# Two groups of seven products instead of one in nine of ten tile pairs, with one of the sums on GpSimd and the residual kept in DRAM

## The chip, the cores and the metric

The kernel runs on one core of one Trainium2 chip. The metric is the device time of one execution in microseconds. The kernel before takes 963.92 us (median of three runs, 963.87 to 964.64).

## The reference, cut to what matters

The reference is one layer of a decoder: sparse attention, a layer norm, a SwiGLU feed-forward part and a second layer norm, for 256 tokens of 2048 features, all in float32.

```
x = LN(alpha*x + mixer(x))                                   # attention, not touched by the change
x = LN(alpha*x + (silu(x @ w_gate) * (x @ w_up)) @ w_down)   # w_gate, w_up: 2048 x 5632; w_down: 5632 x 2048
```

The change concerns `x @ w_gate` and `x @ w_up` (and, by its buffers, the start of `@ w_down`).

## The kernel before, in words

**Three matmuls for one product.** TensorE multiplies in a reduced float32 format (fp32r). To keep the precision, each operand is split into a high part (a rounded copy) and a low part (operand minus high part), and a product is made of three matmuls: high by high, high by low, low by high. So every piece of weights passes two engines before TensorE can use it: the scalar engine (ACT) writes the high part `w_hi` from the loaded `raw`, then the vector engine (DVE) writes `w_lo = raw - w_hi`. Both work on halves of 128 x 1024 elements. `w_hi` and `w_lo` are rings of four halves: ACT may write half n when TensorE has used half n - 4. All halves are counted through the whole kernel (`hi_done`, `lo_done`, `pe_used`).

**Tiles and pairs.** The 5632 hidden columns are cut into 22 tiles of 256; a tile's gate and up columns stand side by side, 512 columns. Tiles 0 and 1 are made alone (`first_tile`, `tile_1`). Tiles 2 to 21 are made in ten pairs, p = 1 to 10, by `pair(p)` on TensorE, `hi_pair(p)` on ACT and `lo_pair(p)` on DVE. The features are 16 blocks of 128 rows (k tiles).

**Seven products for eight.** For the first four k tiles of a pair, two token halves by two k tiles by two column tiles are taken as a 2 x 2 block product and made with seven products instead of eight (Strassen's scheme in Winograd's form). One half then holds one factor for two such block products ("quads"), and TensorE makes 6 matmuls from it (2 quads by 3). The seven weight factors are b11, T1 = b11 + b12, T2 = T1 + b22, b21, T3 = b12 + b22, b22 and T4 = T2 + b21 (signs by the layout); the four sums are made by DVE in place in `raw` (`t_sum`, L1254), two quads at once. The factors of the tokens' side (`s_t`) are made once, before pair 1, by GpSimd (POOL, L1387 to L1398) and ACT (L831). The other twelve k tiles are "plain": 12 halves of 12 matmuls each. So a pair is 7 + 12 = 19 halves and 7 x 6 + 12 x 12 = 186 matmuls of 512 columns, L1769 (`strassen`) and L1782 (`plain`). Between the products ACT copies partial sums from one PSUM bank to another (`seed`, L851, three in a pair, and L871).

**Work of the tiles.** For each tile ACT applies silu (L816), DVE multiplies by the up part (`gate_up`, L1224), TensorE transposes the result (`turn_hid`, L1738, 4 small matmuls), ACT and DVE split it (`hid_hi` L820, `hid_lo` L1228). In the pairs this stands at fixed places between the halves.

**Loads.** All weights come by the SP engine's DMA queue, in program order, each after a wait on `lo_done`. `raw` has five slots of 2048 elements (two halves). In tile 0, tile 1 and the last matrix slots 0 to 3 are a ring; in the pairs slots 0 to 2 are the plain ring and slots 3 and 4 hold the two quads. The quads of pair 1 wait until DVE has split the last half of tile 1, since slot 3 is still in use by it (the row `DMA raw<-in_w_pairs` in the rows below). The residual stream `xn` stays in SBUF.

**The last matrix.** `hid @ w_down` follows the pairs in four column groups of 24 halves, L1561 on TensorE.

The order on each engine is written out by hand. Within an engine nothing is reordered: an instruction whose wait is open holds up all that stands behind it.

## Time and profile before

| | us |
|---|---|
| median of three runs | 963.92 |
| the profiled execution's own time | 964.98 |
| its span, first to last instruction | 962.8 |
| TensorE (PE) busy in the span | 949.2 |
| DVE busy | 624.6 |
| ACT busy | 486.4 |
| POOL busy | 52.2 |
| mean granted TensorE clock | 0.991 |

A matmul's record overlaps the next one's, so a busy share of 99% tells that TensorE hardly ever waits, and not that each record's length is its cost: the cost of one matmul is read from the chain, where a run of matmuls stands as one piece with its count. The chain that ended last runs from the start of the pairs to the end almost wholly over TensorE.

### The profile page before, as it was taken

How to read it: one execution, taken by the hardware profiler on the slowest of the kernel's cores; microseconds unless marked ns; L12 is line 12 of the kernel's file. 1: busy time of each engine (PE TensorE's matmuls, PEld its weight loads, DVE VectorE, ACT ScalarE, POOL GpSimd, SP SyncE). 2: the span in 40 equal slices, each digit the busy share in tenths (PEclk: the TensorE clock that was granted, in tenths of full speed). 3: DMA queues.
4: the chain of work that ended last, by engine and by line, in shares of the span. 5: the costliest groups of instructions: out<-in, count | busy, mean ns of one | idle time of the engine just before them, and what ended most of it. 6: DMA issues, size and time to landing. Idle time of an engine off the chain costs nothing.

```text
span 962.8 us, 11466 instructions
## 1 busy us (share of the span) xinstructions
PE 949.2 (99%) x4536; PEld 794.4 (83%) x4536; DVE 624.6 (65%) x750; ACT 486.4 (51%) x644; POOL 52.2 (5%) x49
## 2 busy tenths in 40 slices
...
GB/s 364 315 136 175 122 55 214 180 392 88 132 87 262 124 270 166 228 197 152 235 115 268 136 253 185 208 216 133 164 206 288 172 220 180 170 225 168 219 131 88
DMA packets 28147, 183.84 MB, mean 191 GB/s; under 512 B 3136, under 2 KB 3648, under 8 KB 8640
## 3 DMA queue, kind: packets, MB, share of 16 engines
...
q8 instruction: 36, 0.59, 0.2%
q14 instruction: 15, 0.12, 0.0%
q0 software_dynamic: 32, 0.00, 0.0%
...
## 4 chain that ended last, share of the span: by engine, by line
PE 70%; DVE 1%; DMA 0%; ACT 0%; issue 0%; DVEq 0%; ACTq 0%
PE acc L1782 26%; PE acc L1561 25%; PE tp L1782 8%; PE acc L1769 6%; PE tp L1769 4%; PE tp L1738 1%; DMA raw<-in_w_pairs 0%; DVE raw L1254 0%; PE acc L1867 0%; DVE w_lo L1090 0%; DVE w_lo L1242 0%; ACT w_hi L836 0%; ACT w_hi L755 0%; DVE stats L1326 0%; ACT acc L851 0%
## 5 line engine op out<-in xcount | busy, mean ns | idle before, releaser
L1090 DVE TENSOR_TENSOR w_lo<-raw,w_hi 128x1024 fp32r<-128x1024 f32 (+1 forms) x123 | 146.1, 1195 | 133.8 <-ACT w_hi L755 133.1
L1782 PE MATMUL acc<-w_hi,act_t 128*128 128x512 f32 x720 | 227.1, 392 | 0.0
L1561 PE MATMUL acc<-w_hi,hid_t 128*128 128x512 f32 x672 | 207.9, 389 | 0.0
L1249 DVE TENSOR_TENSOR w_lo<-raw,w_hi 128x1024 fp32r<-128x1024 f32 x120 | 145.2, 1224 | 95.8 <-ACT w_hi L845 94.7
L755 ACT ACTIVATE w_hi<-raw 128x1024 fp32r<-128x1024 f32 x116 | 115.9, 1001 | 164.7 <-PE acc L1561 152.3
L845 ACT ACTIVATE w_hi<-raw 128x1024 fp32r<-128x1024 f32 x120 | 126.1, 1060 | 126.3 <-PE acc L1782 111.2
L1782 PEld LDWEIGHTS acc<-w_hi,act_t 128*128 128x128 f32 x720 | 135.2, 188 | 27.8
L1561 PEld LDWEIGHTS acc<-w_hi,hid_t 128*128 128x128 f32 x672 | 126.1, 188 | 26.1
L1782 PE MATMUL acc<-w_lo,act_t 128*128 128x512 f32 x360 | 140.2, 389 | 0.0
L1561 PE MATMUL acc<-w_lo,hid_t 128*128 128x512 f32 x336 | 130.7, 389 | 0.0
L836 ACT ACTIVATE w_hi<-raw 128x1024 fp32r<-128x1024 f32 x70 | 72.9, 1057 | 74.4 <-DVE raw L1254 48.5
L1242 DVE TENSOR_TENSOR w_lo<-raw,w_hi 128x1024 fp32r<-128x1024 f32 x70 | 83.9, 1222 | 35.1 <-ACT w_hi L836 34.0
L1782 PEld LDWEIGHTS acc<-w_lo,act_t 128*128 128x128 f32 x360 | 67.7, 188 | 13.6
L1782 PE MATMUL tp<-w_hi,act_t 128*128 128x512 f32 x240 | 74.7, 389 | 0.0
L1561 PEld LDWEIGHTS acc<-w_lo,hid_t 128*128 128x128 f32 x336 | 63.1, 188 | 13.1
L1561 PE MATMUL acc<-w_hi,o_t 128*128 128x512 f32 x224 | 73.4, 398 | 0.0
L1782 PEld LDWEIGHTS tp<-w_hi,act_t 128*128 128x128 f32 x240 | 45.1, 188 | 9.3
L1561 PEld LDWEIGHTS acc<-w_hi,o_t 128*128 128x128 f32 x224 | 42.1, 188 | 8.6
L1254 DVE TENSOR_TENSOR raw<-raw 128x1024 f32<-128x1024 f32 x40 | 47.9, 1219 | 0.0
L1782 PE MATMUL tp<-w_lo,act_t 128*128 128x512 f32 x120 | 46.7, 389 | 0.0
L1561 PE MATMUL acc<-w_lo,o_t 128*128 128x512 f32 x112 | 43.6, 390 | 0.0
L1769 PE MATMUL acc<-w_hi,act_t 128*128 128x512 f32 x100 | 36.9, 410 | 6.6 <-DVE w_lo L1242 6.6
...
## 6 DMA issues: line engine op xcount, KB each, us to landing
raw<-in_w_pairs SPq DMA_DIRECT2D x80, 1024.0 KB, 4.7
raw<-in_w_down SPq DMA_DIRECT2D x32, 1024.0 KB, 4.6
raw<-in_w_out SPq DMA_DIRECT2D x16, 1024.0 KB, 4.8
...
raw<-in_w_gu SPq DMA_DIRECT2D x8, 1024.0 KB, 7.0
...
raw<-in_w_uq SPq DMA_DIRECT2D x4, 1024.0 KB, 6.3
raw<-in_w_ukv SPq DMA_DIRECT2D x4, 1024.0 KB, 5.7
```

The lines of the kernel that those rows point to most:

```text
L755: act.activation(w_hi[:, (2 * slot + half + shift) % RING, 0:n], raw[:, slot, first:first + n], ACT.Copy).then_inc(hi_done, 1)
L836: act.activation(by_quad(w_hi[:, v_pair(p, n) % RING, :]), quad(block), ACT.Copy).then_inc(hi_done, 1)
L845: act.activation(w_hi[:, v_pair(p, n) % RING, :], raw[:, slot, h % 2 * HALF:(h % 2 + 1) * HALF], ACT.Copy).then_inc(hi_done, 1)
L1090: dve.tensor_tensor(w_lo[:, h, 0:n], raw[:, slot, first:first + n], w_hi[:, h, 0:n], ALU.subtract).then_inc(lo_done, 1)
L1242: dve.tensor_tensor(by_quad(w_lo[:, v % RING, :]), quad(block), by_quad(w_hi[:, v % RING, :]), ALU.subtract).then_inc(lo_done, 1)
L1249: dve.tensor_tensor(w_lo[:, v % RING, :], raw[:, h // 2 % PAIR_RING, h % 2 * HALF:(h % 2 + 1) * HALF], w_hi[:, v % RING, :], ALU.subtract) ...
L1254: dve.tensor_tensor(quad(dst), quad(x), quad(y), ALU.add).then_inc(t_done, 1)
L1561: last = pe.matmul(acc[:, bank0 + t, :], lhs[:, k, x, t * P:(t + 1) * P], part[:, w, n * GC:(n + 1) * GC], start=(start and x == 0 and par ...
L1738: last = pe.transpose(turned[:, c, t * P:(t + 1) * P], hid[:, t, c * P:(c + 1) * P], ident[:])
L1769: last = pe.matmul(out, factor(q, what, x), part[:, v % RING, q * GC:(q + 1) * GC], start=(start and (q, x) == (0, 0) and part is w_hi), s ...
L1782: last = pe.matmul(out[:, t, :], act_t[:, k0 + m, x, t * P:(t + 1) * P], part[:, v % RING, m * GC:(m + 1) * GC], start=False, stop=((h % P ...
```

## The change

Pairs 2 to 10 take two groups of four k tiles by the seven products; pair 1 keeps one group (`GROUPS_OF`). A pair of two groups has 14 product halves and 8 plain halves, 22 halves and 14 x 6 + 8 x 12 = 180 matmuls. For each factor the halves of group 0 and group 1 follow each other.

`raw` has six slots: two hold plain halves, four at a time and each with a semaphore of its own (`plain_full`), the other four hold the quads. The two quads of pair 1 go to slots 4 and 5, which tile 1 doesn't use, and their loads have no wait. From pair 2 the quads of the next pair are loaded one by one between plain halves 4 to 7 of the pair before.

GpSimd makes T3 = b12 + b22 in place (`t3_sums`, L1456 of the new kernel), once for each group, after DVE's T1; DVE makes the other three sums of each group (L1312). The tokens' factors of the second group are made in the plain part of pair 1 (`factors_hi(1)` and GpSimd's loop).

`s_t` is twice as large and lies where `xn` lies. `xn` is stored to the DRAM of the output before `s_t` is written (`x1_stored`, waited for by ACT), and loaded back after the products of pair 10 (`x1_back`, waited for by DVE in column group 1 of the last matrix).

In a pair, `turn_hid(2p-2)` moves from the start of the plain part to behind the first product half, `turn_hid(2p-1)` to the start of the plain part; ACT's and DVE's work on the tiles (`hid_chores`) moves to halves 5, 5G+4 and the last of the pair (G is the number of groups).

```diff
-QUADS = 2
-PAIR_K = 2 * QUADS
+QUADS = 4
 B11, B21, B12, B22 = range(4)
+T1, T2, T4 = range(3)
...
+GROUPS_OF = (None, 1) + (2,) * (PAIRS - 2)
 PRODUCTS = 7
-PLAIN = (KD - PAIR_K) // 2
-PAIR_HALVES = PRODUCTS + 2 * PLAIN
-PAIR_RING = 3
-PLAIN_LOADS = PLAIN
-PAIR_SIGNALS = PAIR_HALVES - 2
+PLAIN_SLOTS = 4
...
-        raw = sb("raw", [P, PAIR_RING + QUADS, RAW_ELEMS])
+        raw = sb("raw", [P, PLAIN_SLOTS // 2 + QUADS, RAW_ELEMS])
...
+        s_t = nc.alloc_sbuf_tensor_at("s_t", [P, 2, 4, QUADS, P], F32R, offset=base_x)
...
-        s_t = sb("s_t", [P, 2, 4, QUADS, P], F32R)
...
-                if p > 1:
-                    sp.wait_ge(lo_done, v_pair(p - 1, PRODUCTS))
-                for q in range(QUADS):
-                    if p == 1 and q == 0:
-                        sp.wait_ge(lo_done, V_FFN + 2 * TILE_HALVES)
-                    sp.dma_start(raw[:, PAIR_RING + q, :],
-                                 w_pairs[p - 1][:, q * RAW_ELEMS:(q + 1) * RAW_ELEMS])\
-                      .then_inc(raw_full[PAIR_RING + q], 16)
+            def load_quad(p, n):
+
+                q = quad_slots(p)[n]
+                if p == 1:
+                    pass
+                elif p == 2 and q < 2:
+                    sp.wait_ge(lo_done, V_FFN + TILE_HALVES + 2 * (PLAIN_SLOTS // 2 + q) + 2)
+                else:
+                    sp.wait_ge(lo_done, v_pair(p - 1, products(p - 1)))
+                sp.dma_start(raw[:, PLAIN_SLOTS // 2 + q, :], w_pairs[p - 1][:, n * RAW_ELEMS:(n + 1) * RAW_ELEMS])\
+                  .then_inc(quad_full[q], 16)
...
-                if n >= PAIR_RING:
-                    sp.wait_ge(lo_done, v_pair(p, PRODUCTS + 2 * (n - PAIR_RING) + 2))
-                elif p > 1:
-                    sp.wait_ge(lo_done, v_pair(p - 1, PRODUCTS + 2 * (n + PAIR_RING) + 2))
+                m = PLAIN_BEFORE[p] + n
+                if m < PLAIN_SLOTS:
+                    sp.wait_ge(lo_done, V_FFN + TILE_HALVES + m + 1)
                 else:
-                    sp.wait_ge(lo_done, V_FFN + TILE_HALVES + 2 * n + 2)
-                e0 = (QUADS + n) * RAW_ELEMS
-                sp.dma_start(raw[:, n % PAIR_RING, :], w_pairs[p - 1][:, e0:e0 + RAW_ELEMS])\
-                  .then_inc(raw_full[n % PAIR_RING], 16)
...
+                    sp.wait_ge(lo_done, plain_v(m - PLAIN_SLOTS) + 1)
+                e0 = 2 * GROUPS_OF[p] * RAW_ELEMS + n * HALF
+                sp.dma_start(plain_raw(m), w_pairs[p - 1][:, e0:e0 + HALF]).then_inc(plain_full[m % PLAIN_SLOTS], 16)
...
+                if isinstance(g, int) and n < 2:
+                    sp.wait_ge(lo_done, v_pair(PAIRS - 1, products(PAIRS - 1)))
+                elif isinstance(g, int) and n < RING:
+                    sp.wait_ge(lo_done, V_DOWN - PLAIN_SLOTS + 2 * slot + 2)
                 else:
                     sp.wait_ge(lo_done, V_DOWN + 2 * (n - RING) + 2)
...
+            load_quad(1, 0)
+            load_quad(1, 1)
+            for n in range(PLAIN_SLOTS):
+                load_plain(1, n)
+            sp.wait_ge(x1_done, TOK * CHUNKS)
+            sp.dma_start(a["out"].rearrange("(t p) d -> p t d", p=P), xn[:]).then_inc(x1_stored, 16)
+            for p in range(1, PAIRS):
+                if p > 1:
+                    for n in range(PLAIN_SLOTS):
+                        load_plain(p, n)
+                for n in range(PLAIN_SLOTS, plain_halves(p)):
+                    load_plain(p, n)
+                    if p < PAIRS - 1:
+                        if n - PLAIN_SLOTS < 2 * GROUPS_OF[p + 1]:
+                            load_quad(p + 1, n - PLAIN_SLOTS)
+                    elif n - PLAIN_SLOTS < 2:
+                        load_down(0, n - PLAIN_SLOTS)
+
+            for b in range(2, RING):
                 load_down(0, b)
+            sp.wait_ge(x1_stored, 16)
+            sp.wait_ge(*used_half(v_pair(PAIRS - 1, products(PAIRS - 1))))
+            sp.dma_start(xn[:], a["out"].rearrange("(t p) d -> p t d", p=P)).then_inc(x1_back, 16)
...
+            def factors_hi(g):
+
+                act.wait_ge(x1_stored, 16)
+                act.wait_ge(s_step, 5 * g + 5)
+                act.activation(s_t[:, 0, :, 2 * g:2 * g + 2, :], s_sum[:, g, :, :, :], ACT.Copy).then_inc(s_hi, 1)
...
 
...
+                G, n_products = GROUPS_OF[p], products(p)
+                seeds = {G + 3: (0, first[:, 0, :], 1.0), 3 * G + 3: (2, second[:, 0, :], -1.0),
+                         5 * G + 3: (4, first[:, 1, :], 1.0)}
+                for j in range(halves(p)):
+                    if j in seeds:
+                        if j == G + 3:
+                            act.wait_ge(ffn_hid, 2 * p - 1)
+                        seed(p, *seeds[j])
+                    if j == 2 * G + 4:
+                        if p > 1:
+                            act.wait_ge(p5_added, 2 * (p - 1))
+                        act.wait_ge(*used_half(v_pair(p, 2 * G - 1)))
+                        act.activation(p5_s[:], tp[:, 2, :], ACT.Copy).then_inc(p5_done, 1)
+                    if j < n_products:
+                        hi_product(p, j // G, j % G)
+                    else:
+                        hi_plain(p, j - n_products)
+                    if j == 5:
                         if p > 1:
                             hid_hi(2 * p - 2)
                         silu_step(2 * p - 1)
-                    if h == 9:
+                    if j == 5 * G + 4:
                         hid_hi(2 * p - 1)
+                    if j == n_products + plain_halves(p) // 2 + 3:
                         silu_step(2 * p)
+                    if p == 1 and j == n_products + 6:
+                        factors_hi(1)
...
+            def t_sum(p, g, dst, x, y):
+                dve.tensor_tensor(quad(p, g, dst), quad(p, g, x), quad(p, g, y), ALU.add).then_inc(t_done, 1)
+
+            def hid_chores(p, j):
+
+                if j == 5:
+                    if p > 1:
+                        hid_lo(2 * p - 2)
+                    gate_up(2 * p - 1)
+                if j == 5 * GROUPS_OF[p] + 4:
+                    hid_lo(2 * p - 1)
+                if j == products(p) + plain_halves(p) // 2 + 3:
+                    gate_up(2 * p)
...
+                groups = range(GROUPS_OF[p])
+                for n in range(PRODUCTS):
+                    for g in groups:
+                        lo_product(p, n, g)
+                        if n == 0:
+                            t_sum(p, g, B11, B11, B12)
+                        if n == 3:
+                            t_sum(p, g, B21, B11, B21)
+                        hid_chores(p, GROUPS_OF[p] * n + g)
+                    for g in groups:
+                        if n == 1:
+                            t_sum(p, g, B11, B11, B22)
+                for h in range(plain_halves(p)):
                     lo_plain(p, h)
-                    if h == 3:
...
+                    hid_chores(p, products(p) + h)
+                    if h == 2:
                         dve.wait_ge(p5_done, p)
...
+                    if g == 1 and h == 2:
+                        dve.wait_ge(x1_back, 16)
...
+            def t3_sums(p):
+
+                for g in range(GROUPS_OF[p]):
+                    pool.wait_ge(t_done, T_BEFORE[p] + g + 1)
+                    pool.tensor_tensor(quad(p, g, B12), quad(p, g, B12), quad(p, g, B22), ALU.add).then_inc(t3_done, 1)
...
+            for g in range(2):
+                if g == 1:
+                    pool.wait_ge(lo_done, v_pair(1, products(1)))
+                k = act_t[:, 4 * g:4 * g + 4, :, :].rearrange("p (q k) x s -> p q k x s", q=2)
+                x1, s_g = x1_t[:, g, :, :, :], s_sum[:, g, :, :, :]
+                pool.tensor_tensor(x1, k[:, :, :, 0, :], k[:, :, :, 1, :], ALU.add).then_inc(s_step, 1)
...
+                pool.wait_ge(s_hi, g + 1)
+                pool.tensor_tensor(s_t[:, 1, :, 2 * g:2 * g + 2, :], s_g, s_t[:, 0, :, 2 * g:2 * g + 2, :],
+                                   ALU.subtract).then_inc(s_lo, 1)
+                if g == 0:
+                    t3_sums(1)
+            for p in range(2, PAIRS):
+                t3_sums(p)
...
-                v = v_pair(p, n)
-                pe.wait_ge(lo_done, v + 1)
-                for q in range(QUADS):
-                    for x, part in ((0, w_hi), (0, w_lo), (1, w_hi)):
-                        last = pe.matmul(out, factor(q, what, x), part[:, v % RING, q * GC:(q + 1) * GC],
-                                         start=(start and (q, x) == (0, 0) and part is w_hi),
-                                         stop=((q, x) == (QUADS - 1, 1)), skip_group_check=not start)
-                last.then_inc(pe_used, 1)
+                for g in range(GROUPS_OF[p]):
+                    v = v_pair(p, GROUPS_OF[p] * n + g)
+                    if v == v_pair(p, 1) and p > 1:
+                        turn_hid(2 * p - 2)
+                    pe.wait_ge(lo_done, v + 1)
+                    for n_q in range(2):
+                        for x, part in ((0, w_hi), (0, w_lo), (1, w_hi)):
+                            end = (g, n_q, x) == (GROUPS_OF[p] - 1, 1, 1)
+                            last = pe.matmul(out, factor(2 * g + n_q, what, x),
+                                             part[:, v % RING, n_q * GC:(n_q + 1) * GC],
+                                             start=(start and (g, n_q, x) == (0, 0, 0) and part is w_hi),
+                                             stop=end, skip_group_check=not start)
+                    last.then_inc(pe_used, 1)
...
-                pe.wait_ge(s_lo, 1)
+                pe.wait_ge(s_lo, min(p, 2))
...
-                for h in range(PLAIN):
-                    if h == 0 and p > 1:
-                        turn_hid(2 * p - 2)
-                    if h == 5:
+                n = plain_halves(p) // 2
+                for h in range(n):
+                    if h == 0:
                         turn_hid(2 * p - 1)
                     plain(p, h, first)
```

The order on DVE, from the end of pair 2 into pair 3 (the first L1242 begins pair 3), before. L1242 is the low part of a product half, L1254 a sum, L1249 the low part of a plain half, L1228 `hid_lo` and L1224 `gate_up`:

```order
L1249 TENSOR_TENSOR w_lo<-raw,w_hi 128x1024
L1242 TENSOR_TENSOR w_lo<-raw,w_hi 128x1024
L1254 TENSOR_TENSOR raw<-raw 128x2x512 x2
L1242 TENSOR_TENSOR w_lo<-raw,w_hi 128x1024
L1254 TENSOR_TENSOR raw<-raw 128x2x512
L1242 TENSOR_TENSOR w_lo<-raw,w_hi 128x1024 x2
L1254 TENSOR_TENSOR raw<-raw 128x2x512
L1242 TENSOR_TENSOR w_lo<-raw,w_hi 128x1024 x3
L1249 TENSOR_TENSOR w_lo<-raw,w_hi 128x1024 x4
L1228 TENSOR_TENSOR hid_t<-tp,hid_t 128x2x256
L1224 TENSOR_TENSOR hid<-hid,tp 128x512
```

The same place of the new kernel, the end of pair 2 into pair 3; L1301 is the low part of a product half, L1312 a sum, L1308 the low part of a plain half, L1285 `hid_lo` and L1281 `gate_up`:

```order
L1308 TENSOR_TENSOR w_lo<-raw,w_hi 128x1024 x5
L1281 TENSOR_TENSOR hid<-hid,acc 128x512
L1301 TENSOR_TENSOR w_lo<-raw,w_hi 128x1024
L1312 TENSOR_TENSOR raw<-raw 128x2x512
L1301 TENSOR_TENSOR w_lo<-raw,w_hi 128x1024
L1312 TENSOR_TENSOR raw<-raw 128x2x512
L1301 TENSOR_TENSOR w_lo<-raw,w_hi 128x1024 x2
L1312 TENSOR_TENSOR raw<-raw 128x2x512 x2
L1301 TENSOR_TENSOR w_lo<-raw,w_hi 128x1024 x2
L1285 TENSOR_TENSOR hid_t<-tp,hid_t 128x2x256
L1281 TENSOR_TENSOR hid<-hid,tp 128x512
L1301 TENSOR_TENSOR w_lo<-raw,w_hi 128x1024
```

DVE had four sums among seven product halves, with the work on the tiles behind four plain halves; now it has six among fourteen, and one `hid_lo` and one `gate_up` stand behind the sixth product half.

The SP queue before, from the first loads of the pairs; L521 is a quad and L534 a plain slot of two halves:

```order
L534 DMA raw<-in_w_pairs 128x2048 x3
L521 DMA raw<-in_w_pairs 128x2048 x4
L534 DMA raw<-in_w_pairs 128x2048 x6
L521 DMA raw<-in_w_pairs 128x2048 x2
L534 DMA raw<-in_w_pairs 128x2048 x6
```

The same queue of the new kernel; L559 is a quad, L570 one plain half, L589 the store of `xn`:

```order
L559 DMA raw<-in_w_pairs 128x2048 x2
L570 DMA raw<-in_w_pairs 128x1024 x4
L589 DMA out<-xn 128x2x2048
L570 DMA raw<-in_w_pairs 128x1024
L559 DMA raw<-in_w_pairs 128x2048
L570 DMA raw<-in_w_pairs 128x1024
L559 DMA raw<-in_w_pairs 128x2048
L570 DMA raw<-in_w_pairs 128x1024
L559 DMA raw<-in_w_pairs 128x2048
L570 DMA raw<-in_w_pairs 128x1024
L559 DMA raw<-in_w_pairs 128x2048
L570 DMA raw<-in_w_pairs 128x1024 x9
```

The two quads of pair 1 moved ahead of the plain halves, the store stands behind four of these, and a pair's quads alternate with plain halves, each of which waits for a `lo_done` of its own.

## Rows read from the trace of the kernel before

**Rows 1.** The page: the span, and each engine's busy time.

```profile
span 962.8 us, 11466 instructions
PE 949.2 (99%) x4536; PEld 794.4 (83%) x4536; DVE 624.6 (65%) x750; ACT 486.4 (51%) x644; POOL 52.2 (5%) x49
```

**Rows 2.** The chain of waits in time order: start, us, what. Pairs 1, 2, 10.

```profile
283.60 9.79 PE acc L1769 x30
293.39 13.60 PE acc L1782 x60
...
326.50 4.08 PE tp L1769 x18
...
350.12 0.44 PE tp L1738 x4
...
714.64 2.72 PE acc L1561 x12
```

**Rows 3.** Windows: us, busy of PE, PEld, DVE, ACT, POOL, clock, DMA share, GB/s.

```profile
412.75:455.88 43.13, 43.13 (x196) 35.70 (x195) 30.88 (x29) 23.61 (x28) 0.00 (x0) 1.00 0.51 195
269.99:276.56 6.57, 0.00 (x1) 0.04 (x1) 1.38 (x2) 1.06 (x1) 0.00 (x0) 0.67 0.49 205
276.56:289.30 12.74, 11.49 (x25) 8.12 (x26) 11.39 (x10) 7.60 (x10) 0.00 (x0) 0.50 0.00 0
425.00:426.00 1.00, 1.00 (x6) 0.81 (x5) 0.86 (x2) 0.42 (x1) 0.00 (x0) 1.00 1.02 434
```

**Rows 4.** Timeline of DVE into pair 4, whose first matmul starts at 412.75.

```profile
405.81 1.23 DVE L1242 TENSOR_TENSOR w_lo<-raw,w_hi 128x1024 fp32r<-128x1024 f32 x1 [1.58 <-ACT w_hi L836]
406.95 2.35 DVE L1254 TENSOR_TENSOR raw<-raw 128x1024 f32<-128x1024 f32 x2
409.30 1.23 DVE L1242 TENSOR_TENSOR w_lo<-raw,w_hi 128x1024 fp32r<-128x1024 f32 x1
...
412.78 2.36 DVE L1242 TENSOR_TENSOR w_lo<-raw,w_hi 128x1024 fp32r<-128x1024 f32 x2 [1.13 <-ACT w_hi L836]
```

**Rows 5.** Timeline of ACT there: halves, a seed, a tile's split and silu.

```profile
404.71 1.06 ACT L836 ACTIVATE w_hi<-raw 128x1024 fp32r<-128x1024 f32 x1 [1.74 <-PE acc L1782]
408.20 1.06 ACT L836 ACTIVATE w_hi<-raw 128x1024 fp32r<-128x1024 f32 x1 [2.43 <-DVE raw L1254]
...
414.21 0.58 ACT L851 ACTIVATE acc<-tp 128x512 f32<-128x512 f32 x1 [0.35 <-PE tp L1769]
...
423.28 0.58 ACT L820 ACTIVATE hid_t<-tp 128x512 fp32r<-128x512 f32 x1
423.76 0.59 ACT L816 ACTIVATE hid<-acc 128x512 f32<-128x512 f32 x1
```

**Rows 6.** Timeline of DVE in tile 1 and of `hid_lo`.

```profile
243.85 3.32 DVE L1090 TENSOR_TENSOR w_lo<-raw,w_hi 128x1024 fp32r<-128x1024 f32 x1 [0.26 <-ACT w_hi L755]
...
252.13 0.67 DVE L1224 TENSOR_TENSOR hid<-hid,acc 128x512 f32<-128x512 f32 x1
...
262.42 0.69 DVE L1228 TENSOR_TENSOR hid_t<-tp,hid_t 128x512 fp32r<-128x512 f32 x1 [4.13 <-ACT hid_t L820]
264.31 2.58 DVE L1090 TENSOR_TENSOR w_lo<-raw,w_hi 128x1024 fp32r<-128x1024 f32 x1 [1.20 <-ACT w_hi L755]
```

**Rows 7.** Timeline of POOL: four in a row, then beside tile 1.

```profile
69.22 10.04 POOL L1372 TENSOR_TENSOR more_lo<-raw,more_hi 128x1024 fp32r<-128x1024 f32 x4 [41.06 <-DVE score L1025]
...
243.68 2.41 POOL L1387 TENSOR_TENSOR x_t<-act_t 128x1024 f32<-128x1024 f32 x1 [112.39 <-DVE act_t L1172]
246.16 1.60 POOL L1391 TENSOR_TENSOR s_sum<-x_t 128x256 f32<-128x256 f32 x1
...
263.41 2.40 POOL L1398 TENSOR_TENSOR s_t<-s_sum,s_t 128x1024 fp32r<-128x1024 f32 x1 [10.61 <-ACT s_t L831]
```

**Rows 8.** Timeline of ACT in tile 1: the high part of `s_t`.

```profile
262.28 1.05 ACT L831 ACTIVATE s_t<-s_sum 128x1024 fp32r<-128x1024 f32 x1
```

**Rows 9.** The page: DMA issues, KB each, median us to landing.

```profile
raw<-in_w_pairs SPq DMA_DIRECT2D x80, 1024.0 KB, 4.7
```

More of the change, by code:

```diff
@@ L747, in _, with hi_loop @@
                     hi_static(SPLIT_OF[s])
-            def hi_loop(used, raw_count, half, slot, n=HALF, first=None, shift=0):
+            def hi_loop(used, raw_count, half, slot, n=HALF, first=None):
                 first = half * n if first is None else first
@@ L1811, in pair @@
                 pe.wait_ge(p5_added, 2 * p)
-                for h in range(PLAIN, 2 * PLAIN):
+                for h in range(n, 2 * n):
                     plain(p, h, second)
```

258 lines of the change are left out of this document (114 added, 144 removed).

## The prediction

> **What bounds the kernel now.** I read the page first: TensorE is busy 949.2 of 962.8 us, DVE 624.6, GpSimd 52.2 [rows 1]. Its records overlap, so next comes the chain of waits: from 283.60 on it is TensorE alone. 18 matmuls take 4.08 us, 0.2267 each; a product half (6) is 1.36 and a plain half (12) 2.72; four transposes take 0.44 [rows 2]. Pairs 2 to 10 run from 326.50 to 714.64, nine of 43.13 us: 186 x 0.2267 = 42.17, and two times 0.44; TensorE never waits there. The window of one such pair shows DVE busy 30.88 of 43.13 us and ACT 23.61 [rows 3]: shares that say little of the product part, where TensorE needs a half every 1.36 us and DVE also makes sums.
>
> The windows before pair 1 show the other loss: TensorE stands for 6.57 us, the granted clock goes from 2.4 to 1.2 GHz, and stays there until about 289.3, after 12.7 us of pair 1 [rows 3]. The wait is for pair 1's quads, loaded only when tile 1's last half is split. From the end of tile 1 (269.99) to the first plain half (283.60 + 9.79 = 293.39) pass 23.4 us [rows 2].
>
> The timelines give the steps. Back to back DVE takes 1.14 a step (406.95 to 409.30 for two sums, less 0.07 of overlap), 1.23 alone [rows 4]. An ACT half takes 1.06; it starts 0.12 after TensorE frees the place (half 0 of pair 4: 412.75 - 3 x 2.72 = 404.59, start 404.71) and 0.03 after a sum (408.20) [rows 5]. Seed, `hid_hi` and silu take 0.5 to 0.6 each [rows 5], `hid_lo` and `gate_up` 0.65 each [rows 6].
>
> **The change, part by part.**
>
> TensorE: nine pairs lose 6 matmuls, 54 x 0.2267 = 12.2 us. A pair without a stall would take 180 x 0.2267 + 0.88 = 41.7 us.
>
> Pair 1: its quads are loaded early, so the 6.57 us wait and the slow clock go. What is late next: the low part of tile 1's last half, which starts at 264.31 and ends at 266.89 [rows 6]. DVE then makes half 0 (to 268.0) and T1 (269.1); ACT's half 1 lasts to 270.2, GpSimd's T3 from 269.15 to 271.55, DVE's half 1 ends at 272.65, T2 at 273.8, ACT's half 2 at 274.9 and half 3 at 275.9, the seed that product 2 waits for at 276.5. TensorE starts half 2 there, 3.8 us late, half 4 at 279.7, 0.4 late, and ends half 6 near 284: 23.4 becomes 14, a gain of 9.4 us if the clock holds.
>
> The store of `xn`: ACT's write of `s_t`, at 262.28 [rows 8], now waits for it. It is issued when DVE has split four halves of tile 1, at about 252.2 (`gate_up` starts at 252.13 behind them) [rows 6]; 2 MB at 434 GB/s [rows 3] behind up to 0.5 MB take 6, and landing takes about 2.2 more than moving (4.7 less 2.5 for 1 MB) [rows 9]: 260 to 261. I price it at 0, with 2 us as the upper end. Behind that ACT instruction stands tile 1's last half. The load back has 2.1 MB and stands in SP's queue ahead of the second norm's rows; DVE waits for it a column group later, tens of us. Cost 0, at most 5.
>
> DVE and GpSimd in pairs 2 to 10: here is the price. GpSimd's operation of 128 x 1024 takes 2.40 to 2.41 us with DVE on small operations or on big ones [rows 7]. DVE's does not keep its time: started at 243.85 it took 3.32 us and ended 1.08 after GpSimd's 243.68 + 2.41; that of 264.31 took 2.58 and ended 1.08 after GpSimd's 263.41 + 2.40 [rows 6, 7]. So DVE stood until GpSimd was done. The reverse holds too: a GpSimd step of a quarter of the size took 1.60 at 246.16, while DVE finished its own [rows 7]. `gate_up`, which reads PSUM, took 0.67 at 252.13, as always [rows 6]. The weight splits and the sums all read SBUF twice, so a sum on GpSimd costs DVE up to 2.4 us, where DVE's own sum costs 1.14. For two in a pair: between 0 (they fall in DVE's idle time) and 4.8 us. I take them where they fall in the order.
>
> The Trainium skill, page SBUF — State Buffer, section Who interferes with whom, says that a DVE instruction with two SBUF inputs and a GpSimd instruction that reads SBUF exclude each other, and whoever issues first blocks the other for its whole length. The rows above agree (2.58 for 1.23). By it the whole 2.40 counts; were the port shared half and half, each sum would cost DVE about 1.2 us, and the time would be some 20 us lower. Its page Perfetto Trace Analysis, section Optimizing Scalar/DVE Operations, warns of moving work between these two for this reason.
>
> Now a pair of two groups, time 0 at its first matmul, DVE as in rows 4 at first. Half 0's low part ends at -5.7, T1a at -4.6. GpSimd takes T3a from -4.5 to -2.1, so half 1 ends at -1.0, T1b at 0.1. Half 2 is ready and goes first, to 1.3. T3b runs to 3.7, half 3 ends at 4.7, T2a at 5.9, T2b at 7.0, half 4 at 8.2. TensorE wants half 3 at 4.5 and half 4 at 6.2: stalls of 0.3 and 2.1. Half 5 follows at 9.8 (ACT has a seed first), then `hid_lo` and `gate_up` to 11.0, half 6 at 12.1, T4a, half 7 at 14.4, T4b, half 8 at 16.7. TensorE starts them at 12.2, 14.5 and 16.8, stalls of 1.0, 0.9 and 0.9, plus 0.2 at half 5. From there DVE needs 1.14 a half and TensorE 1.36. The products end at 25.0 for 19.5: 5.5 us of stall. Then `turn_hid` stands at the start of the plain part, ACT waits for it with `hid_hi` and plain half 1 behind it; its low part is ready 0.25 late. Pair: 41.7 + 5.5 + 0.25 = 47.4 us.
>
> From pair 3 loads add to it. In the second part of a pair SP issues 6 MB, each plain half after a `lo_done`; at 434 GB/s they need 14 us and start at 23.5. The last plain half lands near 39.1, where ACT could take it at 36.7; DVE begins the next pair 1.4 us later, misses the idle time before it, and all that follows shifts: 48.8 us. Without this it is 47.4, the other end.
>
> Sum: pair 2 47.4 and eight of 48.8 make 437.8, less 9 x 43.13 = 388.2: +49.6. With pair 1, -9.4: +40.2. On the profiled execution's 964.98 that is 1005.2; the median of the runs lies 1.06 below that execution: 1004.
>
> **The rivals.**
>
> GpSimd's sums cost DVE nothing (they meet its idle time or start behind it). Then half 4 ends at 6.1, `hid_lo` and `gate_up` still hold half 6 until 10.2, and T4a, T4b make halves 7 and 8 late: 0.3 + 1.1 + 0.85 + 0.9 = 3.2 us of stall, with 0.25 behind it: 45.2 a pair, 9 x 2.07 = 18.6, less 9.4, +9: 973. Against it: rows 6 and 7. For it: before the pair DVE does have idle time (1.58 and 1.13 us) [rows 4].
>
> The clock falls in the stalls. For: it fell 2.3 us into the gap before pair 1, by the 0.67 of the 6.57 us [rows 3]. Against: the longest stall here is 2.1 us, and 1.36 us of matmuls lie between. If 1.2 GHz then stays for 12.7 us as in rows 3, halves 4 to 8 take 2 x 1.275 = 2.55 each, to 21.0 instead of 18.2: 2.8 a pair, 25 us: 1029.
>
> DVE keeps up, and it is faster. From the start of half 0's low part (-6.94) to TensorE's start of the last product half (18.1) are 25.0 us, and DVE's 14 halves, 6 sums, `hid_lo` and `gate_up` need 20 x 1.14 + 1.3 = 24.1. If DVE could run that far ahead, the pairs save 12.2, with pair 1 21.6: 942. Against it: four places in the ring, so half 3 can't begin before time 0; DVE would have to have its sums before that, but the order puts T2a and T2b behind half 3. It decides from about 1 us of stall a pair.
>
> **How the numbers follow.** The forecast 0.62 (993 to 1018, by one more or less us a pair and the two prices of the loads); no cost from GpSimd 0.15; the clock 0.15; DVE keeps up 0.05; the rest, between the first two, 0.03. The range 976 to 1028 leaves out the last us of the clock's case, most of the 973 case and the fast one. A measurement tells 0.2% (1.9 us) from no change. Faster 0.05, within 0.2% 0.02, slower 0.93.
>
> **What would show it.** Right: PE's waits for the low part of product halves, about 50 us over the nine pairs, most before halves 4, 6, 7, 8; DVE's longest splits near 2.3 to 3.5 us beside GpSimd's sums; 14 us from tile 1's end to the plain halves at full clock; pairs of 47 to 49 us. Wrong: pairs near 41.7 us, or DVE splits of 1.23 throughout, or clock 0.5 in the products of each pair.

## The result, and the profile after

The changed kernel takes 1012.48 us (median of 4 runs, 1011.13 to 1013.63), the kernel before in the same session 963.89 (4 runs, 963.78 to 964.64). The ratio is 1.0503, with a 95% interval of 1.0486 to 1.0519: 5% slower. The forecast was 1004 us with a range of 976 to 1028.

The page of the changed kernel, to be read against [rows 1]: the span, the busy times, and the shares of the chain that ended last.

```profile
span 1010.7 us, 11576 instructions
PE 955.5 (95%) x4482; PEld 782.0 (77%) x4482; DVE 713.1 (71%) x794; ACT 509.3 (50%) x672; POOL 123.7 (12%) x74
PE 66%; DVE 23%; DMA 6%; ACT 3%; issue 2%; ACTq 0%; DVEq 0%
```

TensorE has the 54 matmuls less, and yet the span is 47.9 us longer. DVE is busy 88.5 us more; the chain, almost wholly TensorE's before [rows 2], now goes to DVE for 23% (1% before) and to transfers for 6%. Where they stand in it, pair 1 and, from the end of pair 4, pair 5:

```profile
287.38 27.25 PE acc L1868 x120
...
464.68 3.33 DVE raw L1312
468.02 4.46 DVE w_lo L1301 x2
484.44 8.41 PE acc L1853 x36
499.62 7.86 DMA raw<-in_w_pairs
```

(Start, us, what, as in rows 2.) The pattern of DVE, DVE, PE and DMA comes back in each of the pairs 3 to 9, and without the DMA in pair 10.

Four of the ten pairs as windows (columns as in rows 3): pairs 2, 3, 5 and 10.

```profile
319.89:367.52 47.63, 43.56 (x189) 34.02 (x188) 39.02 (x35) 26.02 (x30) 5.95 (x2) 1.00 0.45 177
367.52:416.62 49.10, 44.83 (x189) 35.27 (x188) 40.17 (x35) 26.21 (x30) 6.30 (x3) 0.97 0.44 172
466.05:515.35 49.30, 43.63 (x189) 33.94 (x188) 40.64 (x35) 26.03 (x30) 6.76 (x3) 1.00 0.43 171
713.33:762.32 48.99, 44.84 (x189) 35.34 (x188) 38.51 (x34) 25.79 (x30) 3.83 (x2) 0.97 0.40 151
```

Pair 2 takes 47.63 us, pairs 3 to 10 from 48.99 to 50.10; the nine end 442.4 us after pair 2's start, where before they took 388.2 (nine of 43.13 [rows 3]). That is +54.2. Pair 1 gives back 6.4: the first matmul of pair 2 starts at 319.89 instead of 326.34. Together +47.8, the 47.9 of the spans.

Where TensorE stands in pair 5, from its timeline (start, us, engine, line, operation; in brackets the idle time before it and what ended that):

```profile
472.53 0.50 PE L1853 MATMUL tp<-w_hi,s_t 128*128 128x512 f32 x1 [1.62 <-DVE w_lo L1301]
476.11 0.47 PE L1853 MATMUL acc<-w_hi,s_t 128*128 128x512 f32 x1 [1.92 <-DVE w_lo L1301]
479.80 0.50 PE L1853 MATMUL acc<-w_hi,act_t 128*128 128x512 f32 x1 [0.67 <-DVE w_lo L1301]
482.07 0.51 PE L1853 MATMUL acc<-w_hi,act_t 128*128 128x512 f32 x1 [0.61 <-DVE w_lo L1301]
484.44 0.47 PE L1853 MATMUL acc<-w_hi,s_t 128*128 128x512 f32 x1 [0.71 <-DVE w_lo L1301]
```

Each wait is for the low part of a product half (3, 4, 6, 7 and 8), 5.53 us in sum. The idle time understates them: starts of matmuls are 0.2267 apart elsewhere, and against that pace each stall costs 0.16 more than its bracket, and the start behind it comes about 0.1 late again. So counted, the five cost 6.8 us. Waits too short to be listed, above all 0.4 at the second plain half, bring it to 7.4, and 41.7 + 7.4 = 49.1 of the pair's 49.30.

The cause on DVE, and the same stretch on GpSimd (POOL):

```profile
461.19 1.22 DVE L1301 TENSOR_TENSOR w_lo<-raw,w_hi 128x1024 fp32r<-128x1024 f32 x1
462.33 1.22 DVE L1312 TENSOR_TENSOR raw<-raw 128x1024 f32<-128x1024 f32 x1
463.47 1.22 DVE L1301 TENSOR_TENSOR w_lo<-raw,w_hi 128x1024 fp32r<-128x1024 f32 x1
464.60 3.42 DVE L1312 TENSOR_TENSOR raw<-raw 128x1024 f32<-128x1024 f32 x1
467.94 4.54 DVE L1301 TENSOR_TENSOR w_lo<-raw,w_hi 128x1024 fp32r<-128x1024 f32 x2
```

```profile
463.63 3.31 POOL L1456 TENSOR_TENSOR raw<-raw 128x1024 f32<-128x1024 f32 x1 [41.57 <-DVE raw L1312]
468.10 3.30 POOL L1456 TENSOR_TENSOR raw<-raw 128x1024 f32<-128x1024 f32 x1 [1.16 <-DVE raw L1312]
```

GpSimd's first sum starts behind DVE's T1, while DVE is in the split that began at 463.47; DVE's next operation begins at 464.60. The sum ends at 466.94, 2.34 after that, so it lasts 3.31 instead of its usual 2.40 [rows 7], as if it had first waited for DVE. DVE's next sum, begun at 464.60, ends at 468.02, 1.08 after GpSimd's end, in 3.42 instead of 1.22. The two splits behind take 4.54 instead of 2.35 beside the second sum. Against its own times DVE loses 2.2 + 2.2 = 4.4 us in this pair, where making the two sums itself would cost 2 x 1.14 = 2.3.

The end of the pair before, on ACT: the last three plain halves and the first of the next pair.

```profile
450.59 1.07 ACT L903 ACTIVATE w_hi<-raw 128x1024 fp32r<-128x1024 f32 x1 [2.18 <-DMA raw<-in_w_pairs]
454.62 1.06 ACT L903 ACTIVATE w_hi<-raw 128x1024 fp32r<-128x1024 f32 x1 [2.97 <-DMA raw<-in_w_pairs]
458.36 1.06 ACT L903 ACTIVATE w_hi<-raw 128x1024 fp32r<-128x1024 f32 x1 [2.68 <-DMA raw<-in_w_pairs]
459.33 0.58 ACT L859 ACTIVATE hid<-acc 128x512 f32<-128x512 f32 x1
459.80 2.16 ACT L895 ACTIVATE w_hi<-raw 128x1024 fp32r<-128x1024 f32 x2
```

Each of the three waits for its load. The last starts 41.7 us after the pair's start (416.62). In windows over the same stretch (columns as in rows 3) the DMA share goes from 0.38 to full, and back to nothing:

```profile
440.00:445.00 5.00, 5.00 (x26) 4.14 (x25) 2.43 (x3) 1.62 (x3) 0.00 (x0) 1.00 0.38 116
445.00:450.00 5.00, 4.86 (x22) 3.70 (x21) 4.74 (x6) 3.41 (x4) 0.00 (x0) 1.00 0.92 342
450.00:455.00 5.00, 5.00 (x24) 4.14 (x23) 2.65 (x3) 1.45 (x2) 0.00 (x0) 1.00 1.01 414
455.00:460.00 5.00, 5.00 (x24) 4.14 (x23) 1.77 (x2) 2.32 (x4) 0.00 (x0) 1.00 1.01 420
460.00:465.00 5.00, 5.00 (x24) 4.14 (x23) 5.00 (x6) 2.98 (x3) 1.37 (x1) 1.00 0.96 386
465.00:470.00 5.00, 5.00 (x25) 3.96 (x24) 5.00 (x3) 1.06 (x1) 3.84 (x2) 1.00 0.01 3
```

All of a pair's bytes (8 MB) move in some 22 us behind its products, when the four quad slots come free together. While the products run, almost nothing moves (share 0.01).

### The profile page after: what moved, and what is told of

The parts are those of the page before. It is cut to its first block, busy times and chain, and to the rows that moved or that the text cites. A ratio compares the mean times of both kernels' runs of the same rounds, so it can differ in the third digit from the quotient of the medians.

```text
span 1010.7 us, 11576 instructions
## 1 busy us (share of the span) xinstructions
PE 955.5 (95%) x4482; PEld 782.0 (77%) x4482; DVE 713.1 (71%) x794; ACT 509.3 (50%) x672; POOL 123.7 (12%) x74
## 3 DMA queue, kind: packets, MB, share of 16 engines
q1 hardware_dynamic: 34656, 187.32, 48.8%
## 4 chain that ended last, share of the span: by engine, by line
PE 66%; DVE 23%; DMA 6%; ACT 3%; issue 2%; ACTq 0%; DVEq 0%
PE acc L1641 32%; DVE w_lo L1301 11%; DVE raw L1312 7%; DMA raw<-in_w_pairs 6%; PE acc L1868 6%; PE acc L1853 6%; PE acc L1579 5%; PE acc L1500 4%; DVE w_lo L1308 3%; PE tp L1853 3%; PE acc L1778 2%; PE tp L1830 2%; ACT w_hi L895 1%; PE acc L1613 1%; PE tp L1868 1%
## 5 line engine op out<-in xcount | busy, mean ns | idle before, releaser
L1301 DVE TENSOR_TENSOR w_lo<-raw,w_hi 128x1024 fp32r<-128x1024 f32 x133 | 181.2, 1387 | 7.8 <-ACT w_hi L895 7.8
L1165 DVE TENSOR_TENSOR w_lo<-raw,w_hi 128x1024 fp32r<-128x1024 f32 x92 | 103.8, 1132 | 115.9 <-ACT w_hi L955 115.1
L1868 PE MATMUL acc<-w_hi,act_t 128*128 128x512 f32 x512 | 162.9, 393 | 1.3
L1308 DVE TENSOR_TENSOR w_lo<-raw,w_hi 128x1024 fp32r<-128x1024 f32 x84 | 103.4, 1253 | 58.3 <-ACT w_hi L903 58.0
L1868 PEld LDWEIGHTS acc<-w_hi,act_t 128*128 128x128 f32 x512 | 96.1, 188 | 24.7 <-DVE w_lo L1308 5.1
L1456 POOL TENSOR_TENSOR raw<-raw 128x1024 f32<-128x1024 f32 x19 | 60.9, 3207 | 360.7 <-DVE raw L1312 360.7
L1868 PE MATMUL acc<-w_lo,act_t 128*128 128x512 f32 x256 | 99.8, 390 | 0.0
L1853 PE MATMUL tp<-w_hi,s_t 128*128 128x512 f32 x196 | 71.4, 423 | 27.9 <-DVE w_lo L1301 27.9
L1312 DVE TENSOR_TENSOR raw<-raw 128x1024 f32<-128x1024 f32 x57 | 86.2, 1525 | 0.0
L1853 PEld LDWEIGHTS tp<-w_hi,s_t 128*128 128x128 f32 x196 | 39.1, 199 | 46.3 <-DVE w_lo L1301 16.8
L1853 PE MATMUL acc<-w_hi,act_t 128*128 128x512 f32 x188 | 67.4, 407 | 6.5 <-DVE w_lo L1301 6.4
L1147 DVE TENSOR_TENSOR w_lo<-raw,w_hi 128x1024 fp32r<-128x1024 f32 x31 | 42.4, 1383 | 18.8 <-ACT w_hi L798 18.8
L1868 PEld LDWEIGHTS acc<-w_lo,act_t 128*128 128x128 f32 x256 | 48.1, 188 | 9.5
L1853 PEld LDWEIGHTS acc<-w_hi,act_t 128*128 128x128 f32 x188 | 36.0, 191 | 19.9 <-DVE w_lo L1301 12.5
```

Of the source, the lines that this page charges most:

```text
L1165: dve.tensor_tensor(dst, raw[:, slot, half * HALF:half * HALF + n], src_hi, ALU.subtract).then_inc(lo_done, 1)
L1301: dve.tensor_tensor(by_quad(w_lo[:, v % RING, :]), quad(p, g, LOW_OF[n]), by_quad(w_hi[:, v % RING, :]), ALU.subtract).then_inc(lo_done, 1)
L1308: dve.tensor_tensor(w_lo[:, v % RING, :], plain_raw(PLAIN_BEFORE[p] + h), w_hi[:, v % RING, :], ALU.subtract).then_inc(lo_done, 1)
L1312: dve.tensor_tensor(quad(p, g, dst), quad(p, g, x), quad(p, g, y), ALU.add).then_inc(t_done, 1)
L1456: pool.tensor_tensor(quad(p, g, B12), quad(p, g, B12), quad(p, g, B22), ALU.add).then_inc(t3_done, 1)
L1853: last = pe.matmul(out, factor(2 * g + n_q, what, x), part[:, v % RING, n_q * GC:(n_q + 1) * GC], start=(start and (g, n_q, x) == (0, 0, 0 ...
```

## The experiments

Before is 964.49 us in the call of e1 to e4, 964.09 in that of e5 to e8, 963.75 in that of e9 and e10, 963.40 in that of e11 and e12 (medians of 7 or 13 runs). A ratio is to it, with its 95% interval. Where a difference is said to be by the ratios, it is the difference of two ratios times 964; pairs are measured in the trace of the profiled execution.

### e1: b12 + b22 by DVE

```diff
                         if n == 0:
                             t_sum(p, g, B11, B11, B12)
+                            dve.tensor_tensor(quad(p, g, B12), quad(p, g, B12), quad(p, g, B22), ALU.add).then_inc(t3_done, 1)
...
-            for p in range(2, PAIRS):
-                t3_sums(p)
```

> As the changed kernel, but DVE makes T3 too, right behind each T1; GpSimd makes none. Theory (GpSimd's sum stands in DVE's way for its whole 2.4 us, DVE's own costs 1.14): the two T3 of a pair cost 2 x 1.14 instead of up to 2 x 2.4, half 4 is ready about 2.4 us earlier, pairs of about 46.9 us for 49.2, total 1012.5 - 9 x 2.4 = 991 (985 to 997). Rival (the length of DVE's own queue is the trouble, GpSimd's sums cost it nothing): two more sums a pair, + 9 x 2.3 = 1033.

Measured: 994.58 us, ratio 1.0316 (1.0299 to 1.0333). Against the change's 1.0503 that is 18 us less. By the traces the nine pairs are 16.6 us shorter, 1.8 each, where 4.4 less 2.3 of the reading above makes 2.1. The rest lies in pair 1, part of it in a wait for the store that the edit doesn't touch (below). DVE has 19 operations more, and the kernel is faster for it.

### e2: b12 + b22 left out

```diff
-                elif n == 4:
-                    act.wait_ge(t3_done, T_BEFORE[p] // 3 + g + 1)
...
-                t3_sums(p)
```

> As the changed kernel, but T3 isn't made by any engine and product 4 takes b12 as it is (this part of the computation is left out). It tells what T3 costs wherever it is made. Theory: 4.8 us of blocking a pair go, of which some 3.6 show, since part lay in idle time: pairs near 45.7 us, 980 (973 to 988); the difference to the kernel with T3 on DVE is about 1.1 to 2.3 us a pair. Rival (GpSimd's sums cost nothing): 1012 as the changed kernel.

Measured: 979.59 us, ratio 1.0155 (1.0134 to 1.0175), by the ratios 33.5 us less than the change; by the traces the nine pairs are 31.8 us shorter, 3.5 each. That is the whole price of the two sums where GpSimd makes them. It still isn't faster than before. Pair 2, whose loads aren't late, lasts 45.49 us and six of the eight others 45.46 to 45.50, so the late loads hardly show any more; what is left is DVE's other steps, with listed waits of 0.67, 0.62 and 0.70 us before halves 6, 7 and 8.

### e3: an eighth of each quad's bytes from pair 3 on

```diff
-                sp.dma_start(raw[:, PLAIN_SLOTS // 2 + q, :], w_pairs[p - 1][:, n * RAW_ELEMS:(n + 1) * RAW_ELEMS])\
+                w = RAW_ELEMS if p < 3 else RAW_ELEMS // 8
+                sp.dma_start(raw[:, PLAIN_SLOTS // 2 + q, 0:w], w_pairs[p - 1][:, n * RAW_ELEMS:n * RAW_ELEMS + w])\
```

> As the changed kernel, but from pair 3 each load of a quad brings only an eighth of its columns (the rest of the weights is left out, the instructions and waits stay). Theory: the last plain halves and the quads then land in time, DVE starts the next pair earlier, 1.4 to 1.9 us a pair over eight pairs: 1012.5 - 13 = 999 (995 to 1003), pairs 3 to 9 like pair 2 (47.6). Rival (the loads' lateness is taken up by the ring): 1012.

Measured: 998.40 us, ratio 1.0350 (1.0329 to 1.0370). By the ratios 14.7 us less; by the traces the eight pairs are 13.8 us shorter, 1.7 each. In the changed kernel pair 2, whose loads aren't late, was 1.7 us shorter than the mean of the others: the same size from another side. ACT's waits for loads fell from 67.5 to this:

```profile
ACT w_hi L904 <- DMA raw<-in_w_pairs: 31.7, 17, 2.2
```

(Between 310 and 760 us: us in total, times, longest.)

### e4: one group in all pairs

```diff
-GROUPS_OF = (None, 1) + (2,) * (PAIRS - 2)
+GROUPS_OF = (None,) + (1,) * (PAIRS - 1)
```

> As the changed kernel, but all ten pairs take one group of seven products (186 matmuls a pair, as before); buffers, early quads of pair 1, residual in DRAM and T3 on GpSimd stay. It tells the second group's part from the rest's. Theory: pair 1 keeps its gain of 6 us; with one group GpSimd's single T3 falls mostly into DVE's idle time, up to 0.9 us a pair of stall before the seventh half: 958 to 967. Rival (moving the work on the tiles and finer loads cost by themselves): over 975.

Measured: 965.74 us, ratio 1.0013 (1.0004 to 1.0023): the second groups carry the loss. But pair 1's gain, 8.7 us here (pair 2 starts at 317.60 for 326.34), doesn't show either: pairs 2 to 10 last 44.20 us each instead of 43.13. One listed wait of 0.4 us a pair is for the split behind `hid_lo` and `gate_up`; before it, the split beside GpSimd's sum takes 2.44 us instead of 1.22 and sets DVE's row back. Another start is some 0.4 late and not listed. In pair 1 TensorE stands twice:

```profile
272.39 0.47 PE L1853 MATMUL tp<-w_hi,s_t 128*128 128x512 f32 x1 [1.53 <-DVE w_lo L1301]
275.96 0.50 PE L1853 MATMUL acc<-w_hi,s_t 128*128 128x512 f32 x1 [1.95 <-ACT acc L908]
```

### e5: as e4, all sums on DVE, the store of x1 first

```diff
+            sp.wait_ge(x1_done, TOK * CHUNKS)
+            sp.dma_start(a["out"].rearrange("(t p) d -> p t d", p=P), xn[:]).then_inc(x1_stored, 16)
             for n in range(PLAIN_SLOTS):
                 load_plain(1, n)
-            sp.wait_ge(x1_done, TOK * CHUNKS)
-            sp.dma_start(a["out"].rearrange("(t p) d -> p t d", p=P), xn[:]).then_inc(x1_stored, 16)
```

(and e1's and e4's edits)

> One group in all pairs as in e4 (965.7 us), and two more edits: b12 + b22 by the vector engine right behind T1 instead of GpSimd, and the store of x1 issued ahead of tile 1's plain loads. My theory: what e4 lacks of its gain in pair 1 is the lock between GpSimd's sum and DVE's steps (TensorE's stalls of 1.53 and 1.95 us there) and ACT's wait of 1.4 us for the store. Each sum of DVE costs 1.14 us instead of up to 2.4 in which DVE stands: e4's nine waits of 0.4 us (3.6 together) go, pair 1 gains 2 to 4 us more, and the time is 957 to 960. Rival: DVE is simply late in pair 1 with its 1.14 us steps, whoever makes the sum; then 963 to 966.

Measured: 958.35 us, ratio 0.9938 (0.9922 to 0.9955), the fastest of all that were run, level with e11. A window across two of its pairs:

```profile
500.00:543.10 43.10, 43.10 (x194) 1.00 0.54 195
```

(us, PE busy, clock, DMA share, GB/s.) No wait of TensorE is listed in pairs 2 to 10. A pair lasts 43.47 us, 0.73 less than e4's, for one sum moved back to DVE. The 0.34 over the 43.13 of before lie at three product halves, whose first matmuls start about 0.1 us late each (493.20, 497.47, 500.36); what holds them wasn't asked. In pair 1 the first of the two stalls is 0.33 instead of 1.53; the second, 1.96, stays. Yet pair 1 brings only 0.3 us (pair 2 starts at 317.29 for 317.60), where I expected 2 to 4: in e4 ACT didn't wait for the store, so there was nothing to win by the store's place, and pair 1 starts 0.9 us later in this execution.

### e6 and e7: two groups in a better order, without and with GpSimd

```diff
-                        if n - PLAIN_SLOTS < 2 * GROUPS_OF[p + 1]:
-                            load_quad(p + 1, n - PLAIN_SLOTS)
+                    for b in ((0,), (), (1,), (2, 3))[n - PLAIN_SLOTS] if n - PLAIN_SLOTS < 4 else ():
+                        if p < PAIRS - 1 and b < 2 * GROUPS_OF[p + 1]:
+                            load_quad(p + 1, b)
...
-                if j == 5:
+                if j == products(p) + 1:
...
-                if j == 5 * GROUPS_OF[p] + 4:
+                if j == products(p) + 5:
...
-                        if n == 3:
+                        if n == 5:
                             t_sum(p, g, B21, B11, B21)
...
-                    if h == 0:
+                    if h == 2:
                         turn_hid(2 * p - 1)
```

(the same two places for ACT, and e5's order of the store; e6 also has e1's edit)

> Two groups in pairs 2 to 10 as in the changed kernel, all its sums on DVE (b12 + b22 behind T1), and four moves: each quad load goes between plain loads in the order in which ACT asks for the slots (four plain, quad, two plain, quad, one plain, two quads), the store of x1 ahead of tile 1's plain loads, the second pair of T4 sums behind product half 5, and hid_lo, gate_up, the turn of hid_t and hid_hi moved out of the product halves to plain halves 1, 2 and 5. My theory (the stalls are DVE's in the products, the rest late loads): a pair has 41.7 us of TensorE and about 0.6 of stall, 42.3; nine save 7.5 us on before, pair 1 saves 8 to 9, and the time is 946 to 950. Rival: DVE needs 14 steps of 1.14 us and more in 19.5 us of products however they lie, and its lead from the plain halves is used up: 44 us a pair, 962 to 966.

> As e6, but b12 + b22 stays on GpSimd, twice a pair. It tells what the lock alone costs where nothing else is late. My theory: in each pair DVE stands up to 2.4 us for each of the two sums and would have used 1.14 for its own, so it is 2.5 us later; the lead from the plain halves may hide part. 0.5 to 2.5 us a pair, 5 to 22 us over e6: 952 to 970. Rival (the order was all that mattered, the lock lies in idle time): within 3 us of e6.

Measured: e6 961.89 us, ratio 0.9978 (0.9968 to 0.9987); e7 986.32, ratio 1.0248 (1.0217 to 1.0279). By the medians e7 is 24 us over e6, by the ratios 26, so 2.7 to 2.9 a pair; the traces have 2.3 (of e6 the slowest of ten executions was profiled, 964.84). That is more than the 5 to 22 us that I expected, and more than e1's 1.8 a pair; that it is because DVE has no other slack here is not shown. In e7:

```profile
452.68 2.39 POOL L1456 TENSOR_TENSOR raw<-raw 128x1024 f32<-128x1024 f32 x1 [38.83 <-DVE raw L1312]
```

```profile
453.53 2.62 DVE L1301 TENSOR_TENSOR w_lo<-raw,w_hi 128x1024 fp32r<-128x1024 f32 x1 [0.93 <-ACT w_hi L895]
```

Here GpSimd's sum is first and takes 2.39, and DVE's split beside it ends 1.08 after it again.

e6 missed its 946 to 950: its pairs take 43.3 to 44.2 us, not 42.3. Two waits a pair are left, before halves 4 and 12:

```profile
455.97 0.47 PE L1850 MATMUL acc<-w_hi,s_t 128*128 128x512 f32 x1 [1.01 <-DVE w_lo L1301]
467.99 0.47 PE L1850 MATMUL acc<-w_hi,act_t 128*128 128x512 f32 x1 [0.86 <-DVE w_lo L1301]
```

Between the two splits that end them DVE stops only 0.39 us. My rival named that, at 962 to 966: DVE's splits and sums don't fit in the products, however they lie, and its lead from the plain halves is used up.

### e8: the order of the loads alone

The first part of e6's diff, on the changed kernel.

> The changed kernel with one edit: quad loads lie between the plain loads in the order in which ACT asks for the slots, the bytes are the same. My theory: the last plain half lands 1.4 to 1.9 us earlier, which DVE then has at the start of the next pair; eight pairs: 11 to 15 us less, 998 to 1002. e3, which moved an eighth of the bytes of the quads, gave 14 us and is the upper end. Rival: the queue is late by its bytes (6 MB at about 430 GB/s in the second part of a pair), and the order changes nothing: 1010 to 1013.

Measured: 1007.57 us, ratio 1.0452 (1.0435 to 1.0470): 4.9 us less, where I expected 11 to 15. The last plain half does come earlier, but now ACT waits for the second group's quads:

```profile
454.87 1.06 ACT L903 ACTIVATE w_hi<-raw 128x1024 fp32r<-128x1024 f32 x1 [2.73 <-DMA raw<-in_w_pairs]
455.84 0.58 ACT L859 ACTIVATE hid<-acc 128x512 f32<-128x512 f32 x1
456.32 1.05 ACT L895 ACTIVATE w_hi<-raw 128x1024 fp32r<-128x1024 f32 x1
459.89 1.06 ACT L895 ACTIVATE w_hi<-raw 128x1024 fp32r<-128x1024 f32 x1 [2.53 <-DMA raw<-in_w_pairs]
```

So the loads are late mostly by their bytes; the rival (1010 to 1013) was nearer. Of the 4.9 us, 1.3 lie ahead of pair 2, where ACT's wait for the store is 0.67 us in this execution and 1.38 in that of the changed kernel.

### e9, e10, e11: two groups in every other pair

```diff
-GROUPS_OF = (None, 1) + (2,) * (PAIRS - 2)
+GROUPS_OF = (None,) + tuple(2 - p % 2 for p in range(1, PAIRS))
...
+                if early:
+                    load_quad(p + 1, 0)
+                    load_quad(p + 1, 1)
```

All three have e6's other edits, and the first two quads of a pair of two groups wait for the products two pairs back. e10 moves b12 + b22 behind T2; e11 gives the pairs of one group e5's order (`if n == (3 if len(groups) == 1 else 5)` for T4, and so for the tiles' work).

> As e6 (all sums on DVE, the four moves), but only the even pairs have two groups, the odd ones one, and a pair of one group, which uses two of the four quad slots, lets the next pair's first two quads load during its products. In e6 a pair has 41.7 us of TensorE's work and about 2.4 of stall, because all 8 MB of a pair's loads move in 20 us after its products and DVE starts the next pair late; e5's pairs of one group have no stall (43.1). My theory: with two quads loaded early the pairs of two groups start in time; five of them cost 42.0 to 42.6 and save 2.5 to 5.5 us on e5 (958.4): 953 to 956. Rival: DVE's number of steps in the products is the bound whatever the loads do; then a pair of two groups still costs 44.1, the time is 5 us over e5: 962 to 964.

> As e9, with the two sums b12 + b22 behind T2 instead of behind T1, where product 4 needs them six halves later. Theory: in e6 the first stall (0.85 us at half 4) stands behind T1, T3 and T2 in one row; with T3 later half 4 is in time, and what DVE still lacks shows at half 12. If DVE's start is early enough nothing is lacking: 0 to 3 us under e9. Rival: half 5 and the seed then come late instead: the same as e9 within 1 us.

> As e9 (961.5 us), but the pairs of one group keep e5's order (T4 behind product 3, hid_lo, gate_up and the turn of hid_t where the changed kernel has them), the pairs of two groups keep e9's. Theory: the 0.61 us (once 1.29) at the last product's seed in the pairs of one group come from T4 made late, and go, with the slow start behind each: 3 to 4 us. The 0.8 us at half 12 of the pairs of two groups stay: 957 to 959, no better than e5 (958.4), which has no second group at all. Rival: the stall only moves into the next pair, which DVE then begins late; 960 to 962.

Measured: e9 961.52 us, ratio 0.9979 (0.9969 to 0.9988); e10 974.64, ratio 1.0110 (1.0093 to 1.0127); e11 958.49, ratio 0.9950 (0.9934 to 0.9967). e9's theory (953 to 956) failed: early loads do take away the first of e6's waits, the second stays at 0.8 us, and the pairs of one group got one of 0.6 from the late T4. e11 took that away as expected, and is level with e5. e10 failed outright, by my own placing: T2 and the moved sums of both groups now stand in a row ahead of half 4.

```profile
417.29 0.47 PE L1857 MATMUL tp<-w_hi,s_t 128*128 128x512 f32 x1 [2.31 <-DVE w_lo L1308]
429.05 0.47 PE L1857 MATMUL acc<-w_hi,act_t 128*128 128x512 f32 x1 [0.60 <-DVE w_lo L1308]
```

In e11 the pairs of two groups last 43.3 us, those of one group 43.5 to 44.0: of the 1.36 that six matmuls are worth, 0.2 is left. 0.8 goes to the listed wait and 0.2 to the slow starts at it; the rest are starts too little late to be listed, such as e5's pairs have too.

### e12: e6 without its order of loads and of the store

> The changed kernel with all sums on DVE (as e1, 994.6 us) and the work on tiles and T4 moved as in e6, but the quads loaded behind the plain halves and the store of x1 behind tile 1's plain loads, as in the changed kernel. It tells which of the moves gave e6 its 33 us over e1. Theory: the order on DVE and ACT gave most of it, since e8 had only 5 us from the order of the loads: 965 to 970. Rival: late loads cost what they do once DVE isn't late by itself; the loads of quads behind all plain halves then cost 1.5 us a pair or more: 975 to 985.

Measured: 977.41 us, ratio 1.0147 (1.0130 to 1.0164). That is the rival's range, not the 965 to 970 of my theory. By the ratios, e1 and e6 are 32.6 us apart: half, 16.3, comes from moving the tiles' work and T4, half from the order of the loads and the store. The same order of loads gave only 4.9 in e8, where DVE was late anyway: the two causes seem to cover each other, and taking away one shows the other. What late loads cost is no constant: in e12 pair 2, whose loads aren't late, lasts 43.3 us and the later ones 45.7 on the mean, 2.4 more, against 1.7 in the changed kernel and nothing in e2.

## Why the prediction was right

Slower, by the mechanism named, inside its range; the forecast was 8.5 us too low. Of these, 4.6 lie in pairs 2 to 10 and 3.0 in pair 1, both misses to the same side; the rest lies behind the pairs and in the distance between the profiled executions and the medians.

- **The forecast's mechanism: GpSimd's sums stop DVE.** Right, and tested from three sides (e1, e2, e7 against e6). The Trainium skill's page SBUF — State Buffer, section Who interferes with whom, calls it an exclusive lock in which the loser fully blocks; the 3.42 and 4.54 us agree, and so does GpSimd's 3.31, which shows it as the loser too. The prediction had that side once, for the second sum of a pair that DVE begins early: "T3b runs to 3.7" behind half 2, and pair 2's ended at 3.66. In the pairs from 3 on, which DVE begins late, both sums start while DVE is in a split; for them it only shifted the whole row.
- **The stalls of the products.** Right in place, before halves 3, 4, 6, 7 and 8, and in size where the loads weren't late: against the pace pair 2 loses 0.3 before half 3, 2.1 before half 4 and 0.9 before each of halves 6, 7 and 8, where I had 0.3, 2.1, 1.0, 0.9 and 0.9. In all that is 5.2 for 5.5. The second plain half is 0.4 late for 0.25. In pair 5 the late loads show at half 3, where 0.3 becomes 1.9. In the brackets the stalls are smaller, 43.3 us over the nine pairs for the "about 50" of the prediction. Pair 2 took 47.63 (47.4 forecast).
- **Late loads.** 1.7 us a pair for the 1.4 forecast, in the trace and by e3. ACT took the last plain half 41.7 us into the pair, for 39.1 forecast: the products end later as well (26.8 us into pair 4 for 25.0), so the loads begin later.
- **Sum of the pairs.** +54.2 for +49.6: 0.2 of the 4.6 from pair 2, the rest from pairs 3 to 10 (mean 49.35 for 48.8).
- **Pair 1.** The most mis-sized term: 6.4 us for 9.4. Tile 1 ends at 271.77, 1.8 after the 269.99 of before. Most of this is ACT's wait of 1.38 us for the store, which I had priced at 0 with 2 as the end. It differs between executions with the store in the same place: 0.67 us in e8, 0.17 in e1, none in e3 and e4. So that e5, with the store ahead of the plain loads, has none either doesn't show that its place did it. From the end of tile 1 to that of the products pass 15.2 us, 14.0 forecast. The two stalls are 1.54 before half 1 and 1.94 before half 2, where I had 3.8 before half 2 and 0.4 before half 4; but the clock did not hold. From 279.72 to 283.08 eight starts are about 0.42 apart, which is the lower level of 1.2 GHz, and that costs 3.36 - 8 x 0.2267 = 1.5 us.
- **The clock's rival.** It fell, but not as the rival had it. Pairs 3, 6, 8 and 10 show 0.97 as their mean, the others from 2 on 1.00; and they last 49.10, 49.16, 49.31 and 48.99 us, those at full clock 49.30 to 50.10 from pair 4 on. In e3 it is plainer: pairs 3 to 5 at 1.00 and pairs 6 to 10 at 0.96 all last 47.61 to 47.65. Where DVE sets the pace a slow TensorE only fills its own waits.
- **GpSimd costs nothing (973).** Its pair was to last 45.2 us. e2, where nobody makes these sums, has pairs of 45.5, at 979.6.
- **DVE keeps up (942).** No version came there; e6, with the order mended and no GpSimd, comes to 961.9. The reason given against it, four places in the ring, would hold e6, e9 and e11 back as well; whether a larger ring frees them was not tried.
